# Scan levels within 64-token quadrants, as pairs of 64x64 TensorE column tiles

## The reference, cut to what matters

```python
def step(state, inp):
    qb, kb, fb, vb = inp
    b = jnp.cumsum(fb, axis=2)
    ...
    diff = b[:, :, :, None, :] - b[:, :, None, :, :]
    decay = jnp.exp(jnp.where(incl, diff, -jnp.inf))
    scores = jnp.einsum('nhtk,nhsk,nhtsk->nhts', qb, kb, decay)
    intra = jnp.einsum('nhts,nhsv->nhtv', scores, vb)
```

## Time and profile before

| | |
|---|---|
| time, median of 3 runs | 1884.05 us (1883.6 to 1887.24) |
| profiled execution: its time | 1885.56 us |
| profiled execution: its span | 1883.7 us |
| PE busy in the span | 98% |
| the scan's heads | 724 to 888 us of the span |
| matmul records of L2036 | 288 |

### The profile page before, as it was taken

How to read it: one execution, slowest core, us unless ns; L and a number is a source line. 1 busy time by engine, 2 the same in 40 slices (tenths; PEclk the granted TensorE clock), 3 DMA queues, 4 the chain that set the end, 5 groups by cost and what they waited for, 6 DMA issues and landing times.

```text
span 1883.7 us, 32317 instructions
## 1 busy us (share of the span) xinstructions
PE 1853.5 (98%) x11238; PEld 1602.5 (85%) x11238; DVE 1401.9 (74%) x2658; ACT 1042.4 (55%) x1817; POOL 331.4 (18%) x145
## 2 busy tenths in 40 slices
PE   9999999999999999999999999999999999999998
PEld 7877887788888889999999998888888888888887
DVE  7785566667655568898997678977999976666666
ACT  6666455656644466667555555565665543333333
POOL 0000000000000000000000168886777400000000
PEclk9999999999999999999999999999999999999999
DMA  6624655443455544443445445554444455555554
GB/s 217 224 78 148 216 174 178 145 146 124 146 189 189 187 147 157 147 135 124 136 145 175 155 143 181 186 189 152 162 157 161 155 187 192 196 191 191 196 193 156
DMA packets 86157, 314.11 MB, mean 167 GB/s; under 512 B 9568, under 2 KB 9696, under 8 KB 85856
## 3 DMA queue, kind: packets, MB, share of 16 engines
q1 hardware_dynamic: 86048, 312.65, 49.2%
HBM read 311.56 MB, written 1.05 MB: 166 GB/s over the span
## 4 chain that ended last, share of the span: by engine, by line
PE 83%; DVE 13%; ACT 2%; issue 2%; DMA 0%; SPq 0%; DVEq 0%; ACTq 0%
PE ps L424 24%; PE ps L409 14%; PE ps L2735 11%; PE ps L290 6%; PE ps L1967 6%; PE ps L2739 6%; PE ps L2537 3%; DVE wsplit L273 3%; PE ps L819 2%; PE ps L2036 2%; PE ps L2923 1%; DVE sq L2979 1%; PE ps L440 1%; ACT wsplit L267 1%; DVE work L2300 1%
## 5 line engine op out<-in xcount | busy, mean ns | idle before, releaser
L267 ACT ACTIVATE wsplit<-ring 128x1024 fp32r<-128x1024 f32 x572 | 603.8, 1059 | 450.5 <-PE ps L424 265.4
L273 DVE TENSOR_TENSOR wsplit<-ring,wsplit 128x1024 fp32r<-128x1024 f32 x440 | 541.5, 1235 | 304.8 <-ACT wsplit L267 303.8
L424 PE MATMUL ps<-wsplit,gsplit 128*128 128x512 f32 x1992 | 456.5, 390 | 0.0
L424 PEld LDWEIGHTS ps<-wsplit,gsplit 128*128 128x128 f32 x1992 | 373.2, 188 | 81.3 <-issue 4.0
L273 POOL TENSOR_TENSOR wsplit<-ring,wsplit 128x1024 fp32r<-128x1024 f32 x132 | 317.2, 2404 | 664.5 <-ACT wsplit L267 664.2
L2735 PE MATMUL ps<-hsplit,wsplit 128*128 128x512 f32 x1024 | 368.6, 403 | 0.0
L409 PE MATMUL ps<-wsplit,hsplit 128*128 128x512 f32 x1248 | 298.1, 394 | 4.5 <-DVE wsplit L273 3.4
L2739 PE MATMUL ps<-hsplit,wsplit 128*128 128x256 f32 x1024 | 286.4, 280 | 0.0
L409 PEld LDWEIGHTS ps<-wsplit,hsplit 128*128 128x128 f32 x1248 | 231.6, 188 | 55.5 <-DVE wsplit L273 7.3
L290 PE MATMUL ps<-hsplit,wsplit 128*128 128x256 f32 x1956 | 253.6, 287 | 2.6 <-DVE hsplit L340 1.5
L290 PEld LDWEIGHTS ps<-hsplit,wsplit 128*128 128x128 f32 x1956 | 239.8, 191 | 10.4 <-issue 4.5
(11 more groups left out here) (346 smaller groups left out, 1900.3 us busy)
## 6 DMA issues: line engine op xcount, KB each, us to landing
ring<-in_weights SPq DMA_DIRECT2D x572, 512.0 KB, 3.3
work<-in_weights SPq DMA_DIRECT2D x8, 512.0 KB, 5.8
work<-in_tables SPq DMA_DIRECT2D x1, 1995.0 KB, 9.8
work<-in_decay SPq DMA_DIRECT2D x2, 512.0 KB, 5.0
work<-in_subkeys SPq DMA_DIRECT2D x2, 512.0 KB, 4.4
out_x<-work SPq DMA_DIRECT2D x4, 256.0 KB, 2.4
gains_x<-in_x SPq DMA_DIRECT2D x3, 256.0 KB, 6.1
work<-in_small SPq DMA_DIRECT2D x1, 591.0 KB, 8.1
```

Of the source, the lines that this page charges most:

```text
L267: act.activation(wsplit[:, n % RING, 0, :], slab(s), ACT.Copy).then_inc(S("split", "lead"), 1)
L273: eng.tensor_tensor(wsplit[:, n % RING, 1, :], slab(s), wsplit[:, n % RING, 0, :], ALU.subtract).then_inc(S("split", RESTS[stream][0]), 1)
L424: mm = pe.matmul(YR[:, tt, half * 512:(half + 1) * 512], gsplit[:, slot, b, tt * P:(tt + 1) * P], wsplit[:, n, a, half * 512:(half + 1) * ...
```

## The change

Steps 0 to 7 only ever use scores with key and query in the same half of 128 tokens; steps 0 to 6 use only those in the same quarter of 64 tokens, and step 7 only those in neighbouring quarters. The new kernel makes just those 64x64 blocks:

- TensorE: at k = 0 to 7 the two 128x128 products become four 64x64 ones. Each has 64 keys as stationary columns and 64 queries as moving columns, over 128 channels. The products for the first and second 64 keys go to PSUM partitions 0 to 63 and 64 to 127 of the same bank, which are two different column tiles of the array. Step 8 is as before.
- VectorE: steps 0 to 6 are kept in a compact tile `near` of 128 partitions x 2 x 64. Step 0 is a plain copy, steps 1 to 6 are predicated copies of half the former size. Step 7 has none.
- ScalarE: per head two copies put `near` into the quadrants of `sT`, and two put step 7's blocks there straight from PSUM, ahead of the copy of step 8. Each is of 64 partitions x 128 elements.
- TensorE no longer waits for `kept` before a head's output; it waits for `scores` alone.
- The masks are six of 128x64 in place of seven of 128x128. The space in SBUF is padded, so that nothing else moves.

```diff
-            dst = ps[:, 3 + 2 * (k % 2), 0:T].rearrange("p (a c) -> p a c", a=2)
...
-                pe.wait_ge(S(st, "kept"), h * (LEVELS + 1) + (k - 1))
+                pe.wait_ge(S(st, "kept"), h * LEVELS + (k - 1))
...
             for a in range(2):
-                b = 1 - a if k > LEVELS else a
-                mm = pe.matmul(dst[:, a, :], k_[:, a * P:(a + 1) * P], q_[:, b * P:(b + 1) * P], start=True, stop=True)
+                ka, qa_, qb = k_[:, a * P:(a + 1) * P], q_[:, a * P:(a + 1) * P], q_[:, (1 - a) * P:(2 - a) * P]
+                if k > LEVELS:
+                    mm = pe.matmul(level_bank(k)[:, a * P:(a + 1) * P], ka, qb, start=True, stop=True)
+                    continue
+                for h2 in range(2):
+                    mm = pe.matmul(level_tiles(k)[half(h2), a, :], ka[:, half(h2)], qa_[:, half(1 - h2 if k == LEVELS else h2)],
+                                   start=True, stop=True)
...
         pe.wait_ge(S(st, "scores"), h + 1)
-        pe.wait_ge(S(st, "kept"), (h + 1) * (LEVELS + 1))
...
+        act.wait_ge(S(st, "kept"), (h + 1) * LEVELS)
+        for h2 in range(2):
+            act.activation(quadrants(h2, h2), near[half(h2), :, :], ACT.Copy)
+        act.wait_ge(S(st, "level"), (h + 1) * (LEVELS + 2) - 1)
+        for h2 in range(2):
+            act.activation(quadrants(h2, 1 - h2), level_tiles(LEVELS)[half(h2), :, :], ACT.Copy)
         act.wait_ge(S(st, "level"), (h + 1) * (LEVELS + 2))
-        act.activation(strided(sT, P, [[1, T]]), ps[:, 3, 0:T], ACT.Copy).then_inc(S(st, "scores"), 1)
+        act.activation(strided(sT, P, [[1, T]]), level_bank(LEVELS + 1), ACT.Copy).then_inc(S(st, "scores"), 1)
...
-        if k > LEVELS - 2:
-            v.wait_ge(S(st, "kept"), h * (LEVELS + 1) + k)
-        src = ps[:, 3 + 2 * (k % 2), 0:T].rearrange("p (a c) -> p a c", a=2)
-        if k == 0:
-            ins = v.tensor_tensor(diag, src, eye.unsqueeze(1).to_broadcast([P, 2, P]), ALU.mult)
+        if k == LEVELS - 1:
+            v.wait_ge(S(st, "kept"), h * LEVELS + k)
+        if k:
+            ins = v.copy_predicated(near, level_masks[:, k - 1, :].unsqueeze(1).to_broadcast([P, 2, HD]), level_tiles(k))
         else:
-            ins = v.copy_predicated(diag, level_masks[:, k - 1, :].unsqueeze(1).to_broadcast([P, 2, P]), src)
+            ins = v.tensor_copy(near, level_tiles(k))
...
-        keep_vector(v, st, h, LEVELS)
```

More of the change, by code:

```diff
@@ L183, in build @@
     hT = carve(KC, T)
-    level_masks = carve(LEVELS, P, dt=I32)
+    level_masks = carve(LEVELS - 1, HD, dt=I32)
+    near = carve(2, HD)
+    pos[0] += LEVELS * P - LEVELS * HD - HD
     filt_sum = carve(2, D)
@@ L1937, in build @@
     hv = yb[:, 0:4, :].rearrange("p (t a) n -> p t (a n)", t=TT)
-    diag = strided(sT, 0, [[T + P, 2], [1, P]])
+    def half(h2):
[6 more added lines that the diff above has]
+        return level_bank(k)[:, 0:P].rearrange("p (a c) -> p a c", a=2)
     hy = carve(3, T + 2)
@@ L3324, in shape_tables @@
         out[:, a:a + n] = t[k]
-    s, c = np.meshgrid(pp, pp, indexing="ij")
-    m = [((s >> (l + 1)) == (c >> (l + 1))) & ((s >> l) != (c >> l)) for l in range(LEVELS)]
+    s, c = np.meshgrid(pp % HD, np.arange(HD), indexing="ij")
+    m = [((s >> (l + 1)) == (c >> (l + 1))) & ((s >> l) != (c >> l)) for l in range(LEVELS - 1)]
     return out, np.stack(m, 1).astype(np.int32)
```

## The result

The changed kernel takes 1892.59 us at the median of 6 runs (1890.55 to 1894.78), against 1884.42 for the kernel before in the runs beside it. The ratio is 1.0037, 95% interval 1.0026 to 1.0049: 0.37% slower, where 1890.8 us and 0.36% were forecast.

A forecast was written before the change was run, and what follows sets the result against it. TensorE's queue was taken to bound the heads' stretch. Levels 8.5 us more, heads' ends 1.0 less and last head 0.8 less gave 6.7 more: 1884.05 to 1890.8 us, 0.36% slower, with 1885.5 to 1897 as the 8-in-10 range.

The forecast's parts named there:

- The bound: Heads' stretch, 724 to 888 us: a microsecond more or less in TensorE's queue is a microsecond of the span.
- The level's piece: TensorE, steps 0 to 7: eight 64x64 records in overlapping pairs take 0.39 us with the entry, against 0.45 before.
- The seams: Each level pays 0.16 us entering the 64-column shape and 0.19 going back; 0.133 net per level, 8.5 us over 64.
- The heads' ends: Three heads' ends where TensorE waited for step 7's kept copy: that wait goes, 3 x 0.34 = 1.0 us less.
- The last head: A level there waits 0.9 us for ScalarE's operands; 0.8 of it given back, bounds 0 and 1.0.
- VectorE and ScalarE: Per head VectorE saves about 1.4 us, hardly any on the path; ScalarE's four copies cost 1.2, hidden behind its wait.
- sign that L2045's piece is 0.86 at all heads' ends: Output matmuls in the chain: 0.86 us at all heads' ends, where held ones had 1.10, and no wait for scores.
- The factor of two: Skill page's up to 2x at 64: alone, a level goes from 0.45 to 0.22 us and the kernel wins 14 us.
- vanished seam: Rival at the levels: shape changes cost nothing, a level takes 0.22 us, the kernel 1869 us; chance 7%.
- serial pairs: Rival at the levels: pairs do not overlap, a level takes 0.80 us, the kernel 1905 us; chance 5%.
- late scores: Rival at heads' outputs: ScalarE's copies miss the 2 us window, half uncovered adds 5 us, 1896 us; chance 6%.
- wash: Rival: smaller seams or wider VectorE relief, a level costs 0.45 to 0.50 us, some 1882 to 1886 us; chance 8%.

The follow-up runs named there:

- one_column_tile: The changed kernel with all four matmuls of a level (steps 0 to 7) put to the same column tile; 1906.87 us, ratio 1.0114.
- seams_doubled: The changed kernel with three projection matmuls moved between the two pairs of each level, so each enters and leaves the 64-column shape twice; 1914.31 us, ratio 1.0153.
- the two runs with levels in twos: The changed kernel with steps 0 and 1, 2 and 3 and so on back to back, both slots behind: all heads 1890.53 us, heads 0 to 3 only 1887.6 us.
- step7_by_scalar_only: The kernel before, 128x128 matmuls kept, with step 7's blocks put in place by ScalarE and the output waiting for scores alone; 1884.75 us, ratio 0.9991.

## Why the prediction was right, step by step

- **The bound.** TensorE's queue in the heads' stretch set the time, before and after, and that stretch is 6.8 us longer.
- **The level's piece.** 0.39 forecast, 0.38 measured. That pairs overlap was taken from L922 and L1572; one_column_tile shows it in place.
- **The seams.** 0.16 + 0.19 = 0.35 forecast from the earlier trace rows; 0.336 by seams_doubled, 0.34 by the two runs with levels in twos. This is the term that turned the sign: without it the sum gives 14 us faster from the levels alone. With it, 0.133 per level forecast and 0.134 measured.
- **The heads' ends.** 3 x 0.34 given back forecast, 3 x 0.33 measured, and shown by itself in step7_by_scalar_only.
- **The last head.** 0.8 forecast, 0.82 measured, and the closeness is in part luck. The forecast gave back 0.8 of one wait of 0.9. An estimate from the pieces at their undisturbed lengths (16.3 us before, 17.4 after) gives the head 1.2 us of waits before and 0.3 after: step 8's delay of 0.19 went too, which the forecast had not counted, and the output's delay of 0.18 came new, where it counted none. The forecast named two reasons, TensorE coming later and VectorE's shorter copies. The first is able to do it: in seams_doubled VectorE's copies are those of the changed kernel and only TensorE comes later, and head 7 has no wait left. That removing step 7's copy alone does nothing here was shown too. How much of the 0.82 is due to either was not tried.
- **VectorE and ScalarE.** VectorE saves 7 x 0.451 + 0.424 - 6 x 0.304 - 0.291 = 1.47 us per head (1.4 forecast), nearly all of it off the path. ScalarE pays 1.14 (1.2 forecast). In heads 0 to 6 its wait before the copy of step 8 shrank but held, as forecast. In the last head the copies reach the path: 0.18 us, which the forecast allowed for (up to 0.3) and counted as nothing. Its sign that L2045's piece is 0.86 at all heads' ends with no wait for `scores` failed there.
- **The factor of two.** The Trainium skill's page TensorEngine Tiling (Array Packing) says in Overview that tiling gives up to 2x at 64. The runs agree for what streams (0.61 - 0.16 against 0.38 - 0.16 is 2.0) and not for the level. In section Tiling Modes it says that changing the tiling mode drains the engine. The runs agree that each change costs time, 0.34 us for one entry and exit together; that a drain is what takes it, they do not show.

The rivals: no vanished seam (1.62 for twelve projection records says so), no serial pairs (0.38), no late scores but for 0.18 us in the last head, no wash.

## What to carry to other kernels

By the figures of this kernel, column tiles pay per run of tiled matmuls, not per matmul: a run must save more than about 0.34 us of streaming, here more than 1.5 levels, before it breaks even. So gather tiled work into longer runs, and look at the instructions just behind a run, where part of the price lies. When work is gathered, what feeds the second piece has to be moved ahead of unrelated reads on the feeding engines, or the gain turns into a wait.

## What was not expected of the hardware

Not counted in the forecast was that `scores` comes 0.18 us late in the last head. Two other things were expected, but it could well have been otherwise. The order of the tiles in the code hardly matters: two matmuls of one tile followed by two of the other ran in 0.39 us, like the alternating ones in 0.38. And the price is nearly constant: the forecast took it from 256 moving columns in 64- and 32-column tiles, and it held within 0.02 us for 64 moving columns, in 64, 128 and 32 entries and exits.
